# Streaming encoder step on one core: norm and projection in one stage, index queries by thirds of the tokens, and a top-k by rounds of max8 and match_replace

## What is computed

```python
hn = rmsnorm(x, g_mix)
parts = split_proj(jnp.einsum('btd,dn->btn', hn, w_in))
...
s_ix = jax.nn.relu(jnp.einsum('bqhd,bkd->bqhk', q_ix, k_ix) * (IDX_DIM ** -0.5))
score = jnp.einsum('bqh,bqhk->bqk', w_ix * (N_IDX_HEADS ** -0.5), s_ix)
score = jnp.where(chunk_ok, score, -jnp.inf)
top_val, top_idx = lax.top_k(score, topk)      # 256 keys of a prompt query, 40 of a sample query
```

## Time and profile before

| | us |
|---|---|
| median of 3 runs (3903.22 to 3904.62) | 3903.53 |
| the profiled execution's own time | 3907.19 |
| its span, first to last instruction | 3905.4 |
| TensorE busy with matmuls | 3388.9 |
| VectorE busy | 2494.5 |
| ScalarE busy | 1141.0 |
| GpSimd busy | 160.4 |

### The profile page before, as it was taken

The page is one execution under the profiler, slowest core; times in us unless marked ns, Lnnn a source line. Parts: engine busy times, 40 slices in busy tenths (PEclk is TensorE's granted clock), DMA queues, the critical chain, the costliest instruction groups (busy, mean ns, idle before and its releaser), DMA issues. The chain is left out here.

```text
span 3905.4 us, 58909 instructions
## 1 busy us (share of the span) xinstructions
PE 3388.9 (87%) x21785; PEld 2945.4 (75%) x21785; DVE 2494.5 (64%) x5332; ACT 1141.0 (29%) x2365; POOL 160.4 (4%) x174
## 2 busy tenths in 40 slices
PE   3799892999988999999948999659999799999995
PEld 2688781656658999999947888535566699999994
DVE  3189887575754666655635988766656566665665
ACT  3222221564632111111132222235554311111112
POOL 0201100000000000000011101000000000000000
PEclk7899896998989999999968989879899899999997
DMA  4122222211001111111011222221100111111101
GB/s 143 48 69 81 75 67 76 81 57 48 22 11 60 49 48 35 46 48 48 11 35 55 84 66 80 99 81 61 46 12 24 44 49 38 43 48 48 48 27 46
DMA packets 229803, 210.78 MB, mean 54 GB/s; under 512 B 27430, under 2 KB 215494, under 8 KB 227550
## 3 DMA queue, kind: packets, MB, share of 16 engines
q1 hardware_dynamic: 229598, 208.10, 16.6%
HBM read 159.83 MB, written 44.91 MB: 52 GB/s over the span
## 5 line engine op out<-in xcount | busy, mean ns | idle before, releaser
L1684 PE MATMUL psum<-h_split,gate_up_split 128*128 128x352 f32 x6336 | 1019.9, 322 | 44.2 <-DVE gate_up_split L1798 44.2
L1684 PEld LDWEIGHTS psum<-h_split,gate_up_split 128*128 128x128 f32 x6336 | 1011.9, 188 | 48.2 <-issue 46.5
L1828 DVE TENSOR_TENSOR arena<-arena,psum 128x352 f32<-128x352 f32 x1056 | 513.7, 521 | 318.4 <-PE psum L1684 318.2
L1684 PE MATMUL psum<-hid_split,down_split 128*128 128x352 f32 x3168 | 523.2, 325 | 11.1 <-DVE down_split L1798 11.1
L1684 PEld LDWEIGHTS psum<-hid_split,down_split 128*128 128x128 f32 x3168 | 516.8, 190 | 11.6 <-issue 11.6
L854 PE MATMUL psum<-w_in_split,h_split 128*128 128x256 f32 x3456 | 442.8, 288 | 0.0
L854 PEld LDWEIGHTS psum<-w_in_split,h_split 128*128 128x128 f32 x3456 | 428.2, 193 | 14.4 <-issue 14.4
L1025 DVE TENSOR_SCALAR_CACHE_REDUCE flags<-arena,selection 32x160 uint8<-32x160 f32 (+6 forms) x448 | 386.8, 863 | 16.0
L1318 PE MATMUL psum<-arena 64*128 64x512 f32 (+9 forms) x1040 | 220.9, 529 | 159.1 <-DMA arena<-q_turned 138.5
L856 PE MATMUL psum<-h_split,w_in_split 128*128 128x352 f32 x1872 | 317.4, 333 | 45.9 <-POOL w_in_split L992 45.9
L856 PEld LDWEIGHTS psum<-h_split,w_in_split 128*128 128x128 f32 x1872 | 313.7, 197 | 51.7 <-issue 51.7
(11 more groups left out here) (159 smaller groups left out, 3049.6 us busy)
## 6 DMA issues: line engine op xcount, KB each, us to landing
w_in_raw<-in_w_in SPq DMA_DIRECT2D x28, 1024.0 KB
gate_up_raw<-in_w_gate SPq DMA_DIRECT2D x44, 512.0 KB, 3.7
gate_up_raw<-in_w_up SPq DMA_DIRECT2D x44, 512.0 KB, 4.7
down_raw<-in_w_down SPq DMA_DIRECT2D x44, 512.0 KB, 3.2
arena<-k_turned SPq DMA_DIRECT2D x8, 1184.0 KB, 5.8
k_turned<-arena SPq DMA_DIRECT2D x72, 128.0 KB, 2.1
q_turned<-arena SPq DMA_DIRECT2D x48, 176.0 KB, 1.8
arena<-bias_strips SPq DMA_DIRECT2D x4, 2048.0 KB, 10.4
```

Source lines behind the costliest of these rows:

```text
L1684: ins = nc.tensor.matmul(out, w[i], x[k], start=(first and n == 0), stop=(last and n == 2))
L1828: nc.vector.tensor_tensor(x, x, bank(m, down_bank[p])[:, 0:PIECE], ALU.add).then_inc(s.added, 1)
```

## The change

The norm ahead of the projection moves into `stage_project`, and `stage_norm` stays only for the other two norms.

- The sum of squares is now eight f32 matmuls a third on TensorE (24 in all), which accumulate in PSUM; the adds on VectorE go. Norm, rounding, and the weights' own rounding are interleaved by hand in ScalarE's queue.
- The first three pieces have raw buffers of their own and are loaded at the start of the stage. Their outputs come by thirds of the tokens: for each third one `special` and four index queries. The other pieces keep their order.
- A scoring goes into the queues in chunks of four units, the first up to 10 us ahead of the time at which VectorE is expected to be free, the others one by one between the outputs that follow. The sample block and block 2 no longer have their rest in one run. `block_time` is new.
- `select` is now rounds: `max` gives the eight largest of a row, `match_replace` puts a sentinel in their place, 32 rounds for a prompt block and 5 for the sample block, and one comparison at the end.
- The last block no longer waits for the projections. No flags are moved in `stage_project`: SyncE moves them at the start of `stage_attend`, between the loads of the first queries, and TensorE waits for them at the second and third prompt block that need them.
- Turns use one PSUM bank instead of two. The load of the first attention group is placed by the plan, and waits for all scorings.

```diff
+OUTS_PER_PIECE = 5
+PRODUCT_US = dict(index=3.9, special=3.9, q=3.9, k=3.1, v=3.1)
+SLACK_US = 1
 def block_time(blk):
-    return 31 * (blk.keys / 1300 + 0.55) + 8 * (blk.keys / 960 + 0.2) + 2 * NIX * (blk.keys / 960 + 0.1) * 0.7
+    us = blk.keys / 960
+    weighted = NIX * (us + 0.3)
+    rounds = (TOPK_PROMPT if blk.n < NT else TOPK_SAMPLE) // ROUNDS_OF_8
+    return weighted + rounds * (2 * us + 0.4) + 1
...
+        for i in range(3):
+            for pc in self.pieces[:EARLY]:
+                self.feature_major(pc, i)
...
+            if o.piece.i >= EARLY:
+                if not chunks and waiting and now >= free - 10:
+                    blk = waiting.pop(0)
+                    chunks = self.chunks_of(blk)
+                    plan.append(("score", chunks.pop(0)))
+                    now += 1.5
+                    due = free + SLACK_US
+                    free = max(free, now) + block_time(blk)
+                    begun = blk
+                elif chunks and now >= due:
...
+                    plan.append(("score", chunks.pop(0)))
+                    now += 1.5
...
-            def select(blk, score, flags):
...
-                for bit in range(30, -1, -1):
-                    counted(u, ALU.is_lt, cand)
-                    own(nc.vector.tensor_scalar(step_bits, count, limit, float(1 << bit), ALU.is_ge, ALU.mult))
-                    own(nc.vector.scalar_tensor_tensor(out=cand_bits, in0=step_bits, scalar=(1 << bit) >> 1, in1=cand_bits,
-                                                       op0=ALU.bitwise_xor, op1=ALU.bitwise_xor))
...
+            def select(blk, score):
+
+                top = m.top[0:blk.rows, :]
+                for _ in range((TOPK_PROMPT if blk.n < NT else TOPK_SAMPLE) // ROUNDS_OF_8):
+                    own(nc.vector.max(top, score))
+                    own(nc.vector.match_replace(out=score, in_to_replace=top, in_values=score, imm_value=TAKEN))
+                nc.vector.tensor_scalar(score, score, TAKEN / 2, None, ALU.is_gt).then_inc(s.selected, 1)
...
-                if blk is SELECTED[-1]:
-                    dve.wait_ge(s.proj_done, len(proj))
-                    flags = taken_keys(m)[blk.n]
...
+            for i in range(8):
+                square(i)
             high(0)
+            for i in range(8, 14):
+                square(i)
+            keep_params()
+            rstd(0)
+            for i in range(14, 16):
+                square(i)
+            for i in range(KC):
+                h_high(i)
+            high(1)
+            rstd(1)
+            for i in range(16, 24):
+                square(i)
+            high(2)
+            rstd(2)
+            for i in range(KC, 2 * KC):
+                h_high(i)
...
+            load_q(0)
+            move_flags(masked_blocks[0], s.first_flags_in)
+            for e in range(1, 3):
                 load_q(e)
+            for blk in masked_blocks[1:]:
+                move_flags(blk, s.flags_in)
...
+                    if blk is masked_blocks[0]:
+                        pe.wait_ge(s.first_flags_in, 16)
+                    if blk is masked_blocks[1]:
+                        pe.wait_ge(s.flags_in, 16 * (len(masked_blocks) - 1))
```

More of the change, by code:

```diff
@@ L664, in first_out, with add, feature_major @@
+        self.turns, self.plan, self.units, self.n_units = [], [], {}, 0
+        self.lay_out(list(SELECTED))
+    def add(self, o):
+        self.outs.append(o)
+        self.last_out[o.piece.i] = o.o
+    def feature_major(self, pc, i):
+        for f in range(pc.width // P):
+            self.add(Out(len(self.outs), pc, f, i, i * PIECE, PIECE, self.moved if pc.kind == "q" else 0))
+            self.moved += pc.kind == "q"
     def first_out(self, p):
-        return self.last_out[p - 1] + 1 if p else 0
+        return next(o.o for o in self.outs if o.piece.i == p)
@@ L690, in lay_out @@
             plan.append(("out", o))
-            now += 3.75 if o.piece.kind not in "kv" else 2.8
+            now += PRODUCT_US[o.piece.kind] if o.piece.i >= EARLY else 0
             if o.piece.kind == "k" and o.i > 0:
@@ L702, in lay_out, with chunks_of @@
                 plan.append(("turn", self.turns[-1]))
+            rested += not waiting and not chunks
+            if rested >= 3 and o.o >= last_k and not loaded:
+                plan.append(("load", None))
+                loaded = True
         for blk in waiting:
-            if not begun:
-                self.begin(blk)
-            plan.append(("score", (blk, 1)))
-            begun = False
-    def begin(self, blk):
+            chunks += self.chunks_of(blk)
+        plan += [("score", us) for us in chunks]
+        if not loaded:
+            plan.append(("load", None))
+    def chunks_of(self, blk):
         us = []
@@ L794, in _ @@
                     p = x.i + 1
-                    sp.wait_ge(s.high, p)
-                    sp.wait_ge(s.low, p)
-                    load_piece(m, a, l, pieces[p])(sp, s.raw_in)
+                    if p == EARLY:
+                        sp.wait_ge(s.squares_added, 3 * KC)
+                    else:
+                        sp.wait_ge(s.high, p)
+                        sp.wait_ge(s.low, p)
+                    load_piece(sp, a, l, pieces[p], m.w_raw, s.raw_in)
+                if what == "load":
+                    sp.wait_ge(s.added, plan.n_units)
+                    sp.wait_ge(s.spread, 32)
+                    for r in range(2):
+                        sp.wait_ge(moved[r], 16 * len(range(r, plan.moved, 2)))
+                    wait_moved_up_to(sp, "ds")
+                    n_next = load(sp, s.next_in)
                 if what == "out":
@@ L908, in gates @@
                 pe.wait_ge(s.scanned, 2)
+            sum_squares(0)
+            turn_params()
+            sum_squares(1)
+            sum_squares(2)
             for what, x in plan.plan:
-                if what != "piece":
+                if what not in ("piece", "load"):
                     {"out": out, "turn": turn, "score": score, "gates": gates}[what](x)
```

362 lines of the change are left out of this document (199 added, 163 removed).

## The result

The changed kernel takes 3936.24 us (3932.82 to 3939.04) against 3903.99: a ratio of 1.0082, 95% interval 1.0065 to 1.01. It is slower by 32 us, where 33 us of gain was forecast. Its profiled execution took 3939.04 us, with a span of 3936.8, against 3907.19 and 3905.4 before.

The account below looks back on a forecast made before the run. VectorE's chain of scorings and selections was taken to bound the stage's end. Start -26, selection -11, last wait -12.5, between links +33 gave -16.2 us a layer, -32.5 in all: 3871 us (own range 3845 to 3897).

Parts of the forecast that it names:

- VectorE's chain: Scoring and selection of seven blocks in turn on VectorE set the stage's end, in 659.4 us in place of 675.6.
- the price of a round: In selection, one `max` and `match_replace` round costs 2K/960 + 0.42 us, 2.55 at 1024 keys.
- the flags: Flag moves at the start of `stage_attend` cost 0, with 8 us a layer as the bad end.
- the last wait: The last block's wait for the last projection goes: -12.5 us a layer.
- Rivals 1 to 4: Cheaper rounds 3851 (chance 0.13); dearer rounds 3931 (0.15); passes at half speed 4127 (0.09); `match_replace` held by GpSimd 3905 (0.08).
- rival 2: In selection, dearer rounds with 0.65 us fixed: +30 us a layer, 3931, slower than before; chance 0.15.
- The start of the chain: At the stage's start, VectorE's first scoring begins at 161.5 in place of 187.4: 26 us earlier.
- TensorE's first output starts at 87.3: After the norm, VectorE's scaling and subtraction let TensorE's first output start at 87.3, where it was 111.4.
- Between the selections: Scoring chunks alternating with outputs make VectorE wait between selections: 128 us in place of 95, +33 a layer.
- The length of selections: Seven blocks' selections by rounds take 370 us a layer against 381 by bits: -11.
- The rule for holds: GpSimd's subtraction holds VectorE instructions with two SBUF inputs or in a two-port mode; one-input instructions aren't held, no holds added.
- Rival 5: Early start doesn't reach VectorE, as first blocks' chunks wait for weights: further 10 us a layer, 3891, within the forecast's range.

Follow-up runs that it names:

- two_banks: The changed kernel with two PSUM banks for turns again in place of one: 3907.6 us.
- sums_later: The changed kernel with TensorE's last sum of squares behind its first output and ScalarE's last high part ahead of the last eight squares: 3931.8 us.
- fetch_early: The changed kernel with SyncE issuing the loads of later weight pieces earlier, four outputs into a piece in place of behind all: 3858.7 us.

## Why the prediction was wrong

Right: that VectorE's chain sets the end of the stage, in both layers; that the last selection would lie open with TensorE idle under it for 80 us (86); the price of a round to 0.03 us; that no `max` or `match_replace` is held by GpSimd (rows below); that the flags cost nothing (TensorE uses block 3's 14.1 us after the stage began, 14.3 before); that the last wait goes. Rivals 1 to 4 did not happen. That rival 2's time, 3931, is the nearest to the result is chance, since a round had 0.45 us fixed and not its 0.65.

GpSimd is idle under the last selection, so the holds are read from shorter rows. These are of the changed kernel at 896 keys, during a subtraction; the two passes last what they last without one (1095 and 1076 ns on average):

```profile
544.03 4.59 POOL L1093 TENSOR_TENSOR w_in_split<-w_in_raw,w_in_split 128x2048 fp32r<-128x2048 f32 x1 [31.65 <-ACT w_in_split L1001]
...
545.45 1.09 DVE L1151 MAX8 top<-arena 128x8 f32<-128x896 f32 x1
...
546.66 1.08 DVE L1152 MATCH_REPLACE8 arena<-top,arena 128x896 f32<-128x896 f32 x1
```

Wrong, by its own steps:

- **The start of the chain** (26 us forecast, 20 measured). The step "TensorE's first output starts at 87.3" left out TensorE's own queue: it took h's readiness (85.4 in the trace, forecast 87.3) for the start, while the sixteen matmul records of the last sums, counted as work, stood ahead of it without a time. They could not begin before 85.65, since they wait for ScalarE's last squares, and took 7.9 us; the first output began at 93.15. From there the outputs and turns went as priced (first scoring 74.5 us after the first output, forecast 74.2).
- **Between the selections** (+33 forecast, +56 measured). This is the step that turned the sign: 23 us a layer, 46 in all. The first three blocks were right (forecast 10, 9 and 21.5, measured 9.8, 10.2 and 21.0), then 640 keys took 23.7 for 19.5, 768 took 30.5 for 23, 896 took 35.4 for 28, 1024 took 19.5 for 17. The count knew of chunks behind a late weight and named the hold by the subtraction after the cast. It did not know of the turn that waits for ScalarE's copy behind the same cast (6.2 and 6.0 us). two_banks takes these waits away, and the phases of 768 and 896 keys fall by 3.8 and 7.8, the latter to 27.6, its forecast. That its chain also begins earlier is hardly the reason: in sums_later it begins 2.5 earlier and these phases stay at 30.6 and 35.3. So the missing wait is about half of the 23 us. The other half (4.2 at 640 keys, 3.7 at 768, 2.5 at 1024, and 1.2 by which the prediction took the time before too long) has no experiment of its own. fetch_early shows only that the late loads as a whole are 33 us of the time between the selections, and the prediction had counted some of that.
- **The length of selections** (370 forecast, 375.4 measured): the right mechanism, 0.03 us a round too small. What the change saves here is the sample block and the holds, and nothing else: with their holds taken off, the old selections last 29.7, 40.0, 45.2, 50.3, 55.4, 60.6 and 65.7 us, as the prediction estimated, and the rounds 4.0, 40.4, 49.0, 57.6, 66.2, 74.8 and 83.4.
- **The rule for holds** was put too narrowly. "One-input instructions aren't held" rested on one row of a single element a partition. The earlier trace rows showed the opposite already: VectorE's first scoring instruction has one input and took 4.36 us beside GpSimd's subtraction.
- **Rival 5** had the right mechanism at 3891: the early start not coming through. It was limited to the first blocks, and it was the later ones that waited.

The kind of sum is at fault too. It priced parts of the change one by one, and the experiments show that they lean on each other. The rounds alone cost 30 us in the old order, and taking them out of the new order gave nothing. In the kernel with early loads and two banks the bits for the long rows gave 73. A saving on a link of the chain counts only when the scores of the next link are ready by then, and TensorE's, ScalarE's and SyncE's queues decide that.

## What to carry to other kernels

Where one engine's chain sets the end, write out for each link when its input leaves the other queues, with everything that stands ahead of it there, own matmuls and copies included, before pricing the link. Give a load the place at which its buffer comes free, not that of its consumer's neighbour: a cast that waits for its weight holds everything behind it in ScalarE's queue, relus and copies out of PSUM alike. Choose a top-k by length and by what runs beside it: here, for 256 of K keys, 32 rounds took 32 x (2K/960 + 0.45) + 0.7 us or less, and 31 bits with their ties 0.04 x K + 24.7 where nothing held them (an estimate: the selections above, each less what its held instructions took beyond their usual 0.15 us). That is level at 384 keys, and the bits are shorter beyond. Each hold by GpSimd added 3 to 4.5 us to the bits; with two of them in a selection the kernel before took 58.9 us at 640 keys, where rounds took 57.6, and 63.5 at 768, where they took 66.2.

## What the runs showed of the hardware

The times by form in the changed kernel (count, busy us, mean ns, idle before) are these; from 384 to 1024 keys both passes grow by one element each 1/0.96 ns, which leaves `MAX8` 0.16 and `MATCH_REPLACE8` 0.14 us fixed; loading the eight values takes 92 ns.

```profile
L1151 DVE MAX8 top<-arena 128x8 f32<-128x1024 f32 x32 | 39.3, 1228 | 1.1
L1152 DVE MATCH_REPLACE8 arena<-top,arena 128x1024 f32<-128x1024 f32 x32 | 38.7, 1208 | 0.0
L1151 DVE MAX8 top<-arena 128x8 f32<-128x384 f32 x32 | 18.0, 561 | 1.1
L1152 DVE MATCH_VALUE_LOAD arena<-top,arena 128x8 f32 x192 | 17.7, 92 | 6.6
```

Not expected: the comparison at the end of a selection has one input and takes half as long an element as the passes (0.69 us for 1024, 0.36 for 384), and it is held, though the passes ahead of it aren't. In fetch_early, GpSimd and VectorE:

```profile
282.37 4.49 POOL L1098 TENSOR_TENSOR w_in_split<-w_in_raw,w_in_split 128x2048 fp32r<-128x2048 f32 x1 [22.05 <-ACT w_in_split L1006]
...
282.40 4.75 DVE L1158 TENSOR_SCALAR arena<-arena 128x512 f32<-128x512 f32 x1
```

In the changed kernel the same comparison takes 0.43 us when no subtraction runs (at 301.58). The Trainium skill has this case too ("SBUF — State Buffer", section "SBUF: two separate sides"): a VectorE instruction in a two-port mode takes the shared port pair as well as one with two SBUF inputs. The trace agrees, with 4.75 us here, as far as it goes: it doesn't name the mode, which is read from the halved time an element.
